# Two blocks of a transformer on one core: single buffers in the expert stage, sixteen weight slots, an earlier h copy, and constant products in TensorE's waits

## The reference

```python
def first_block(x, mem, ...):
    for i in range(DEPTH):                      # DEPTH = 2
        ...                                     # i = 0: gated spatial mixing; i = 1: short convolution; both: attention over mem
        o = jnp.concatenate([tok, xa], axis=-1) @ w_out[i]
        x = layer_norm(ALPHA * x + o, ln1_g[i], ln1_b[i])
        f = grouped_moe(x, router_w, router_b, w_gate[i], w_up[i], w_down[i])
        x = layer_norm(ALPHA * x + f, ln2_g[i], ln2_b[i])
    return x

def grouped_moe(x, router_w, router_b, w_gate, w_up, w_down):
    scores = jax.nn.sigmoid(xt @ router_w)      # 16 experts in 4 groups
    ...                                         # one group of each token, then its best two experts
    for e in range(N_EXPERTS):
        h = jax.nn.silu(xt @ w_gate[e]) * (xt @ w_up[e])
        out = out + combine[:, e:e + 1] * (h @ w_down[e])
    return out
```

## Time and profile before

| | |
|---|---|
| median of 3 runs | 1638.48 us (1633.69 to 1639.2) |
| profiled execution | 1635.38 us, of which the span from the first to the last instruction is 1633.6 us |
| mean granted TensorE clock | 0.965 |
| PE busy | 1492.3 us, 91% of the span |
| DVE, ACT busy | 790.6 us (48%), 541.0 us (33%) |
| DMA | 340.25 MB, 51.3% of the sixteen engines' time for the weights' queue |

### The profile page before, as it was taken

How to read it: one execution, slowest core, us unless ns; L and a number is a source line. 1 busy time by engine, 2 the same in 40 slices (tenths; PEclk the granted TensorE clock), 3 DMA queues, 4 the chain that set the end, 5 groups by cost and what they waited for, 6 DMA issues and landing times.

```text
span 1633.6 us, 20733 instructions
## 1 busy us (share of the span) xinstructions
PE 1492.3 (91%) x8792; PEld 1058.0 (65%) x8792; DVE 790.6 (48%) x1144; ACT 541.0 (33%) x835; POOL 25.4 (2%) x35
## 2 busy tenths in 40 slices
PE   6998999997986999996999999999879999999997
PEld 6856444444944444444887786887678776669865
DVE  4724112125534121126687564775367766547743
ACT  4511110113301111113563655442146537444421
POOL 0000000000000000000000000100000000001000
PEclk9998999998998999997999899999899998999999
DMA  8448999993458999992433244002344333240031
GB/s 347 178 189 353 406 396 421 421 420 131 175 206 321 400 421 421 421 421 80 161 126 120 104 154 155 27 1 94 133 156 175 117 109 129 81 178 1 2 116 65
DMA packets 47475, 340.25 MB, mean 208 GB/s; under 512 B 5296, under 2 KB 5296, under 8 KB 7568
## 3 DMA queue, kind: packets, MB, share of 16 engines
q1 hardware_dynamic: 45504, 328.03, 51.3%
q0 software_dynamic: 1872, 10.80, 1.7%
HBM read 337.76 MB, written 1.05 MB: 207 GB/s over the span
## 4 chain that ended last, share of the span: by engine, by line
PE 82%; DVE 12%; ACT 3%; issue 2%; DMA 1%; DVEq 0%; SPq 0%; ACTq 0%
PE bank L498 51%; PE bank L773 14%; PE bank L814 7%; PE bank L717 4%; PE bank L501 3%; DVE d_lo L1621 2%; PE bank L746 1%; PE bank L751 1%; ACT arena L1226 1%; DVE xT_lo L1605 1%; DVE arena L1598 1%; DMA ring<-wsecond 1%; PE bank L540 1%; ACT d_hi L1263 0%; PE bank L799 0%
## 5 line engine op out<-in xcount | busy, mean ns | idle before, releaser
L1621 DVE TENSOR_TENSOR d_lo<-ring,d_hi 128x2048 fp32r<-128x2048 f32 (+2 forms) x96 | 215.4, 2251 | 159.6 <-ACT d_hi L1263 159.4
L498 PE MATMUL bank<-arena 128*128 128x128 f32 (+10 forms) x2016 | 228.4, 285 | 23.5 <-ACT arena L1226 10.3
L1263 ACT ACTIVATE d_hi<-ring 128x2048 fp32r<-128x2048 f32 (+2 forms) x96 | 180.0, 1879 | 163.2 <-PE bank L498 102.4
L498 PEld LDWEIGHTS bank<-arena 128*128 128x128 f32 (+6 forms) x2016 | 195.3, 179 | 49.6 <-issue 23.6
L1226 ACT ACTIVATE arena<-bank 128x512 f32<-128x512 f32 (+3 forms) x222 | 125.2, 581 | 278.6 <-PE bank L498 184.9
L498 PE MATMUL bank<-d_hi,xT_hi 128*128 128x512 f32 (+1 forms) x400 | 164.8, 412 | 10.7 <-DVE xT_lo L1605 10.7
L498 PE MATMUL bank<-xT_hi,d_hi 128*128 128x256 f32 x592 | 168.2, 284 | 5.7 <-DVE d_lo L1621 2.2
L498 PE MATMUL bank<-ring,arena 128*128 128x512 f32 (+2 forms) x384 | 160.9, 578 | 9.0 <-DVE arena L1732 3.4
L498 PE MATMUL bank<-xT_hi,d_lo 128*128 128x256 f32 x592 | 166.9, 282 | 0.0
L498 PE MATMUL bank<-xT_lo,d_hi 128*128 128x256 f32 x592 | 166.5, 281 | 0.0
L498 PE MATMUL bank<-d_hi,xT_lo 128*128 128x512 f32 (+1 forms) x400 | 160.4, 401 | 0.0
(11 more groups left out here) (306 smaller groups left out, 1715.1 us busy)
## 6 DMA issues: line engine op xcount, KB each, us to landing
ring<-wmoe SPq DMA_DIRECT2D x98, 1024.0 KB, 10.6
ring<-wsecond SPq DMA_DIRECT2D x80, 1024.0 KB, 4.6
arena<-wmoe SPq DMA_DIRECT2D x52, 1024.0 KB, 11.2
ring<-wfirst SPq DMA_DIRECT2D x30, 1024.0 KB, 4.7
wide<-wmoe SPq DMA_DIRECT2D x28, 1024.0 KB, 12.7
xT_raw<-wmoe SPq DMA_DIRECT2D x14, 1024.0 KB, 12.5
rows<-lnrows POOLq DMA_DIRECT2D x4, 1024.0 KB, 7.7
ring<-wsecond SPq DMA_DIRECT2D x4, 848.0 KB, 7.8
```

Of the source, the lines that this page charges most:

```text
L498: mark(nc.tensor.matmul(o, lhsT, rhs, start=start, stop=stop, skip_group_check=loose), full)
L1263: nc.scalar.activation(d_hi[h % NHIGH][:, 0:width], raw[u % NRAW][:, 0:width], ACT.Copy).then_inc(sem("piece_high"), 1)
L1621: v.tensor_tensor(d_lo[u % NRAW][:, 0:width], raw[u % NRAW][:, 0:width], d_hi[h % NHIGH][:, 0:width], SUB).then_inc(sem("piece_low"), 1)
```

## The change

Three things are changed.

**Memory.** `now`, `og_hi`, `og_lo` and `hT` have one buffer each instead of two, `sg` is gone (silu writes to `hh`, and DVE multiplies in place), and `now`, `hh`, `hT` move to the place of the memory tokens. With the room that this leaves, `slots` has sixteen entries: 15 in the circle, one used once, and five of them `EARLY`. `put` keeps its two buffers.

**The h copy.** ACT copies the turned h to `hT` right after the first half of the next pair's tokens, and `put` after it.

**Constant products.** `busy(b, n)` waits until bank b is free and multiplies the identity by 512 columns of constants n times into it; nobody reads the result. Such products stand ahead of TensorE's waits for the next tokens, between the halves of a turn, while `xT_lo` is written, and ahead of waits in the router and at the output projection.

```diff
-NSLOT = 13
-NEARLY = 2
+NSLOT = 15
+NEARLY = 1
...
-        RAW_SLOT, HIGH_SLOT = (6, 7, 4, 5), (8, 9, 3)
-        EARLY, NORMED, TOKENS = (0, 1, 2), 10, (11, 12)
+        RAW_SLOT, HIGH_SLOT = (8, 9, 6, 7), (10, 11, 5)
+        EARLY, NORMED, TOKENS = (0, 1, 2, 3, 4), 12, (13, 14)
...
-            def transpose_tokens(src, first, second):
-
+            def busy(b, n):
+
+                pe_eng.wait_ge(bank_free[b], pe.used(b))
+                for _ in range(n):
+                    mm(banks[b][:, :], ident, cst[:, 0:4 * P])
+
+            def transpose_tokens(src, first, second, waiting=0, between=0, after=0):
+
+                if waiting:
+                    busy(5, waiting)
                 for g in range(4):
                     tt, half = g // 2, g % 2
                     if g == 0:
                         pe_eng.wait_ge(sem(first), pe.next(first))
                     elif g == 2 and second != first:
+                        if between:
+                            busy(4, between)
                         pe_eng.wait_ge(sem(second), pe.next(second))
...
+                if after:
+                    busy(4, after)
                 for g in range(4):
                     pe_eng.wait_ge(bank_free[g], pe.used(g))
...
-                    transpose_tokens(x_nat, "x_first", "x_ready")
+                    transpose_tokens(x_nat, "x_first", "x_ready", 4, 2, 2)
...
                 pe_eng.wait_ge(bank_free[3], pe.used(3))
+                if i:
+                    busy(6, 4)
                 pe_eng.wait_ge(bank_free[4], pe.used(4))
                 pe_eng.wait_ge(sem("tok_ready"), pe.next("tok_ready"))
...
-                transpose_tokens(x_nat, "x_first", "x_ready")
+                transpose_tokens(x_nat, "x_first", "x_ready", (0, 7)[i], 0, (2, 2)[i])
...
+                busy(4, 3)
                 pe_eng.wait_ge(sem("chosen_ready"), pe.next("chosen_ready"))
...
                         if p == 0:
+                            busy(4, 1)
                             pe_eng.wait_ge(sem("slots_ready"), i + 1)
...
-                                ins = nc.tensor.matmul(bank[own, :], now[p % 2][:, k, own], w[:, kk, m, :], start=k == 0, stop=k == KD - 1)
+                                ins = nc.tensor.matmul(bank[own, :], now[:, k, own], w[:, kk, m, :], start=k == 0, stop=k == KD - 1)
...
-                transpose_tokens(y_nat, "h_first", "h_ready2")
+                transpose_tokens(y_nat, "h_first", "h_ready2", (13, 5)[l], 0, (2, 6)[l])
...
-                transpose_tokens(merged, "merged_ready", "merged_ready")
+                transpose_tokens(merged, "merged_ready", "merged_ready", 4, 0, 3)
...
+                def turned_comb(p):
+
+                    g = NPAIR * i + p
                     act_eng.wait_ge(sem("gather_full"), 3 * g + 3)
                     nc.scalar.activation(put[p % 2], banks[2][:, 0:T], ACT.Copy).then_inc(sem("put_ready"), 1)
...
                     if p + 1 < NPAIR:
                         tokens(p + 1)
                     act_eng.wait_ge(sem("hT_full"), g + 1)
-                    nc.scalar.activation(hT[p % 2], v3(banks[6][:, :], KM), ACT.Copy).then_inc(sem("hT_ready"), 1)
+                    nc.scalar.activation(hT, v3(banks[6][:, :], KM), ACT.Copy).then_inc(sem("hT_ready"), 1)
+                    if p + 1 < NPAIR:
+                        turned_comb(p + 1)
```

More of the change, by code:

```diff
@@ L238, in two_blocks @@
         bgT = uT
-        now = [v3(arena[:, n * KD * P:(n + 1) * KD * P], KD) for n in range(2)]
         ce = Carve(base1)
         og_at = ce.at
-        ce.at += 4 * D
-        og_hi = [reduced(f"og_hi{b}", arena_at + 4 * (og_at + 2 * b * D), D) for b in range(2)]
-        og_lo = [reduced(f"og_lo{b}", arena_at + 4 * (og_at + (2 * b + 1) * D), D) for b in range(2)]
+        og_hi = reduced("og_hi", arena_at + 4 * og_at, D)
+        og_lo = reduced("og_lo", arena_at + 4 * (og_at + D), D)
+        ce.at += 2 * D
+        pick = ce(TT, NE * SLOTS_OF)
+        assert ce.at <= vv_at
+        ce = Carve(vv_at)
+        tok_slots = [ce(HALF_SLOT) for n in range(2)]
         put = [reduced(f"put{b}", arena_at + 4 * (ce.at + b * T), T) for b in range(2)]
         ce.at += 2 * T
-        pick = ce(TT, NE * SLOTS_OF)
-        sg, hh = ce(F), ce(F)
-        hT = [ce(KM, P) for n in range(2)]
         assert ce.at <= xsc_at
+        ce = Carve()
+        now = ce(KD, P)
+        hh = ce(F)
+        hT = ce(KM, P)
+        assert ce.at <= KD * T
         ce = Carve(memT_at)
@@ L745, in put_pair @@
                             tok = slice(n // 2 * P, (n // 2 + 1) * P)
-                            ins = nc.tensor.matmul(banks[LAST_PUT[n]][:, :], put[p % 2][:, tok], og_hi[p % 2][:, cols], start=not kept, stop=False)
+                            ins = nc.tensor.matmul(banks[LAST_PUT[n]][:, :], put[p % 2][:, tok], og_hi[:, cols], start=not kept, stop=False)
                             carry(ins)
@@ L813, in down @@
                                 own = slice(64 * m, 64 * m + 64)
-                                ins = nc.tensor.matmul(banks[(7, 3)[n]][own, :], hT[p % 2][:, k, own], w[:, n, m, :], start=k == 0, stop=k == KM - 1)
+                                ins = nc.tensor.matmul(banks[(7, 3)[n]][own, :], hT[:, k, own], w[:, n, m, :], start=k == 0, stop=k == KM - 1)
                                 if n == 0 and m == 0:
@@ L1340, in tokens @@
                     act_eng.wait_ge(sem("gather_full"), 3 * g + 1)
-                    nc.scalar.activation(now[p % 2][:, 0:4, :], v3(banks[0][:, :], 4), ACT.Copy).then_inc(sem("tokens_first"), 1)
+                    nc.scalar.activation(now[:, 0:4, :], v3(banks[0][:, :], 4), ACT.Copy).then_inc(sem("tokens_first"), 1)
+                def turned_comb(p):
+                    g = NPAIR * i + p
                     act_eng.wait_ge(sem("gather_full"), 3 * g + 3)
@@ L1350, in _ @@
                         act_eng.wait_ge(sem("h_ready"), g)
-                    nc.scalar.activation(sg, banks[5][:, :], ACT.Silu).then_inc(sem("silu_done"), 1)
+                    nc.scalar.activation(hh, banks[5][:, :], ACT.Silu).then_inc(sem("silu_done"), 1)
                     if p + 1 < NPAIR:
@@ L1360, in _ @@
                         act_eng.wait_ge(sem(("down_first", "down_second")[half]), g + 1)
-                        nc.scalar.activation(og_hi[p % 2][:, half * 512:(half + 1) * 512], banks[b][:, :], ACT.Copy).then_inc(sem("og_first"), 1)
+                        nc.scalar.activation(og_hi[:, half * 512:(half + 1) * 512], banks[b][:, :], ACT.Copy).then_inc(sem("og_first"), 1)
                 act_eng.wait_ge(sem("spill_known"), i + 1)
@@ L1812, in tokens @@
                     dve_eng.wait_ge(sem("gather_full"), 3 * g + 2)
-                    v.tensor_copy(now[p % 2][:, 4:8, :], v3(banks[1][:, :], 4)).then_inc(sem("tokens_second"), 1)
+                    v.tensor_copy(now[:, 4:8, :], v3(banks[1][:, :], 4)).then_inc(sem("tokens_second"), 1)
                     dve_eng.wait_ge(sem("put_ready"), g + 1)
```

17 lines of the change are left out of this document (10 added, 7 removed).

## The result

The changed kernel takes 1609.87 us in the median of 4 executions (1609.84 to 1611.94), the kernel before 1638.84 in the same series (1633.69 to 1640.81). The ratio is 0.983, with a 95% interval of 0.981 to 0.986: 29 us or 1.7% less, clear of the noise, though under 2%. The profiled execution took 1609.85 us with a span of 1608.0. The forecast was 1614, with 1602 to 1624 as the range.

A forecast was written before the change was run, and what follows sets the result against it. TensorE's own work and its waits, many followed by half clock, were taken to bound the kernel. Terms -13.4, 0, -6.5, -6.1, +0.4, +1.0, +1.7 sum to -22.9 us from 1635.4, 1612.5, stated as 1614; range 1602 to 1624.

The forecast's parts named there:

- The h copy: Pairs of both expert stages: the earlier copy removes fourteen 0.96 us waits of the down products, -13.4 us.
- rival C: Expert pairs: the weights bind, so the 13.4 us come back as waits for loads, up to 1627; chance 0.06.
- the margin: Last weight units of the expert stage: they land at least 9 us before the last quarter of down products starts.
- Memory: Single buffers and extra weight slots: costed at 0, since they buy lead for the loads and lead isn't short.
- bound for the single buffers: If a single buffer caused a wait, at most a 0.6 us copy in each of 16 pairs, 10 us.
- Ahead of the expert stages: Work before both expert stages: constant products recover half-clock time, -6.5 us, bounds 0 and -6.8.
- rival B: Ahead of the expert stages: light router and counting products let the clock fall, losing the 6.5 us, 1620; chance 0.18.
- Inside the second block: Turns in the second block: constant products recover half-clock time in three windows, -6.1 us, bounds -3 and -6.1.
- The output projection: At i = 1: products behind the bank 2 wait delay it 2.1 us and get back 1.7, sum +0.4.
- The branches: Behind the two branches: products start only after jumps of 3.8 and 3.3 us, costing +1.0 and +1.7 us.
- Rival A: Behind the branches: the jump costs nothing, products run at once, 9.7 us less, 1604; chance 0.15.
- Rival D: All constant products: they don't bring the clock back, 71 last 1.7 us each, kernel slower at 1682; chance 0.05.

The follow-up runs named there:

- hcopy_only: The kernel before with one edit, ScalarE's h copy placed ahead of its copy to `put`; 1625.19 us, ratio 0.992.
- no_constants: The changed kernel with all constant products taken out, memory and h copy still changed; 1623.86 us, ratio 0.992.
- old_slots: The kernel before with the h copy and constant products of the change, but the old buffers and weight slots; 1612.67 us, ratio 0.984.
- heads_only: The changed kernel with constant products kept only ahead of the expert stages; 1613.55 us, ratio 0.986.
- block2_only: The changed kernel with constant products only at the three later turns inside the second block; 1619.17 us, ratio 0.988.
- constants_only: The kernel before with the constant products added and nothing else; 1631.94 us, ratio 0.997.
- early_in_wo1: The changed kernel with three products ahead of the waits for the output projection's banks, replacing four behind bank 3's; 1610.45 us, ratio 0.984.
- none_after_branch: The changed kernel without the 4 and 13 constant products right behind the two branches; 1603.60 us, ratio 0.979.
- changed_again: The changed kernel measured once more, unchanged, in a later series; 1612.93 us, ratio 0.985.
- ahead_of_branch: The changed kernel with four products ahead of each branch, none left behind the first and nine behind the second; 1603.66 us, again 1604.53.

## Why the prediction was right, and where it was not

**The h copy: right.** Forecast -13.4, seen -14.4 over the pairs of both stages. In place of the earlier trace rows's 0.96 us a pair wins 1.03. Alone it gives 12.0 us in the median (hcopy_only). The weights (rival C) don't bind: TensorE is without a gap over 135 us, and the lead is 9.9 us, about the 9 that the margin was put at.

**Memory: right at 0**, by no_constants against hcopy_only, and by old_slots. The prediction's own bound for the single buffers, 10 us, found no place in its range; nothing hung on it.

**Ahead of the expert stages: right in kind, one stretch left out.** Forecast -6.5, seen -7.7 between the traces, and the windows stand at 1.00 through the light work, so rival B falls. For the second stage the forecast took one window, from 510.4 on. The first of these rows of the kernel before shows another, around the turn, that it left out: 2.83 us of work at half clock, worth 1.4.

```profile
491.70:498.60 6.90, 2.83 (x14) 2.83 (x15) 6.03 (x9) 1.40 (x3) 1.05 (x2) 0.51 0.21 47
498.60:508.70 10.10, 4.49 (x37) 3.40 (x36) 5.15 (x20) 4.43 (x7) 0.00 (x0) 1.00 1.00 412
508.80:515.60 6.80, 5.91 (x28) 5.80 (x28) 3.11 (x9) 0.60 (x1) 0.00 (x0) 0.50 1.02 408
```

The worth of these products isn't a fixed number either. This is the same place in hcopy_only, where nothing but the h copy has changed (this trace is of the slowest of its ten executions):

```profile
486.80:500.50 13.70, 7.90 (x36) 6.12 (x37) 8.02 (x12) 3.88 (x6) 1.04 (x2) 0.50 0.59 231
503.90:514.20 10.30, 7.99 (x37) 7.89 (x38) 4.87 (x18) 0.60 (x1) 0.00 (x0) 0.50 1.00 413
```

TensorE was busy at half clock for 8.7 us there before and is for 15.9 in hcopy_only, a difference of 3.6 us of time. With the products (heads_only) the same place is at 1.00:

```profile
484.00:501.00 17.00, 15.73 (x97) 10.68 (x95) 9.84 (x32) 6.04 (x10) 1.05 (x2) 1.00 1.01 422
```

It is not shown that the h copy makes this difference. At the head of the first stage, ahead of which TensorE's order is the same in all of them, the work at half clock is 8.6 us in the trace of before, 11.5 in hcopy_only, 11.7 in no_constants and 7.6 in block2_only. And over all executions of the series the mean granted clock is 0.962 both before (24 of them) and in hcopy_only (ten). So a sum that reads the half clock from one trace of before takes what this trace happened to have.

The two changes together gave 26 to 29 us, where each alone gave 12.0 and 5.2. About half of that gap of 9 to 12 us is on the side of constants_only: its trace wins 10.2 us at its own places and loses 5.9 elsewhere in the second block. That is not one execution's bad luck, since the mean granted clock of its ten executions is 0.982, against 0.985 and 0.986 in the two series of the changed kernel, which is at most 5 to 7 us of time. Why its clock is lower, and where the rest of the gap comes from, stays open.

**Inside the second block: right.** Forecast -6.1, seen -5.7; block2_only gives 4.7.

**The output projection: right in size.** Forecast +0.4, seen +0.3, by the way that was given: the products start at 447.24, behind the wait for bank 2, and the projection is 2.1 us late. That the place was at fault and not the products is shown by early_in_wo1, where the 2.1 are gone.

**The branches: the sum was right, the reading incomplete.** Forecast +1.0 and +1.7, seen +0.1 and +1.9. Of the 0.9 us at the first, 0.4 is luck: the jump took 3.38 us in this trace and 3.78 in the one of before. The jump of over 3 us is there, the products start behind it, at half clock, and last 5.2 and 13.0 us:

```profile
L864 PEldq COMPARE_BRANCH  x2: 3377/3474/3572, 375.1 to 725.4; - x2
```

Rival A falls with this row. By the Trainium skill, Advanced Engine Details and Errata, section Control Flow Timing, a compare-and-branch takes about 108 ns; in all traces of this case this one took 3.3 to 4.0 us on TensorE, so the trace does not agree. It doesn't either for the other engines that make the same jump, each over its own code: ACT's took 45 ns and DVE's 56 to 72, and DVE is at work again 0.3 us after its branch began. So a long jump is TensorE's alone here, and DVE makes x ready while it lasts. Why TensorE's is so much longer, no run shows. What the prediction didn't see is that its +1.0 was made of two things of opposite sign: two and two products between and behind the halves of the turn, which are worth keeping, and four that only delay. In the traces, the kernel with neither (heads_only) comes to the projection's later products level with the changed kernel, and the one with the former alone (none_after_branch) some 2.8 us ahead of both. It took the change as given and compared it with before. The arithmetic for the other was at hand: the prediction itself has the jump over at 390.3 and says that x is "all but there" at 390.4, so there was no wait left to fill. The turns start 4.6 and 5.0 us later than before, counted from the stage's end, a little under the 5 to 6 forecast.

**Rival D** needed products that don't hold the clock; the head windows at 1.00 are against it.

**The total.** The terms gave -22.9, the traces -25.4. The differences are 1.2 at the heads, 1.0 at the h copy, 0.9 at the first branch and 0.1 at the output projection, less 0.7 at the second branch, the turns and elsewhere. What I left out of the sum, half-clock stretches at other places in the second block, came to nothing in the first trace only because 2.7 us lost and 2.6 won cancel, which is luck; in changed_again it cost 2.7 us.

The best version is ahead_of_branch: 1603.7 and 1604.5 us, 6 to 8 below the changed kernel. none_after_branch is as fast, with seventeen products fewer.

## What to carry to other kernels

Filling a wait of TensorE with products that nobody reads pays when the wait is real and the products end before it does. Before placing them behind a branch, subtract the jump from the wait; what is to run during the jump must be issued ahead of it. Test such fills one place at a time, since a sum that comes out right can hold a place that loses, and read a gain in clock from several executions, because the half-clock stretches of one trace are partly its own.

## What the runs showed of the hardware

- What was issued ahead of a branch goes on running while the sequencer spends 3.3 to 3.9 us in it: eight records from 374.63 to 378.2 over a jump from 374.9 to 378.3.
- The same jump held TensorE's sequencer for 3.3 to 4.0 us in every trace, and took 56 to 72 ns on DVE and 45 ns on ACT.
- Stretches of half clock (0.50 granted) lasted between 3.4 and 17.1 us. Most of those of the second block stand at the same place in two executions of the same program; two of 10.2 us don't. Each of the two begins 2.0 us after an idle gap of 1.27 us, and the same gap in the other execution is not followed by a fall.
- A gap of TensorE of 3.45 us behind a branch was followed by 3.4 us at half clock with four constant products right behind the branch, and one of 4.13 us by the same 3.4 without them. Without products inside the turn too, the half clock lasted 13.7 us.
